# Gated linear attention: a head's square sum behind the next head's first projection, in another bank, and the next arguments ahead of the norm

## What is computed

```python
def _mixer_c(h, s0, with_state, w_in, w2, b2, norm_g, w_out):
    q, k, v, gz, lr = _split(h @ w_in, [H * GLA_DK, H * GLA_DK, H * GLA_DV, H * GLA_DV, 2 * GLA_RANK])
    ...
    o_f, s_f = _gla_chunked(q, k, v, glog[:, :, 0], s0[:, 0])
    o_b, s_b = _gla_chunked(_rev(q), _rev(k), _rev(v), _rev(glog[:, :, 1]), s0[:, 1])
    out = _gated_rms_norm(o_f + _rev(o_b), gz, norm_g) @ w_out

def _gated_rms_norm(o, z, g):
    y = o * lax.rsqrt(jnp.mean(o * o, axis=-1, keepdims=True) + EPS) * g.astype(F32)
    return (y.reshape(B, T, H * V) * jax.nn.silu(z.astype(F32))).astype(z.dtype)
```

## Time and profile before

| | us |
|---|---|
| timed executions, median of three | 1919.06 |
| their lowest and highest | 1918.38, 1927.1 |
| profiled execution, its time | 1928.48 |
| profiled execution, its span | 1926.7 |
| mean granted TensorE clock | 0.901 |

### The profile page before, as it was taken

The page is one execution under the profiler, slowest core; times in us unless marked ns, Lnnn a source line. Parts: engine busy times, 40 slices in busy tenths (PEclk is TensorE's granted clock), DMA queues, the critical chain, the costliest instruction groups (busy, mean ns, idle before and its releaser), DMA issues.

```text
span 1926.7 us, 21105 instructions
## 1 busy us (share of the span) xinstructions
PE 1687.5 (88%) x7872; PEld 1052.5 (55%) x7872; DVE 529.6 (27%) x1288; ACT 474.3 (25%) x865; POOL 147.6 (8%) x188
## 2 busy tenths in 40 slices
PE   5899999979998999798899999588898869999984
PEld 3455688865556888554543333456676545433334
DVE  1564332434634424202200000153232240000002
ACT  2254321222453212103111111143323131111111
POOL 0010011010000111000100000102222000000001
PEclk8899896889998968799899999787999889999997
DMA  9122125122123253015579999420210355999973
GB/s 373 51 82 87 67 110 200 42 110 83 72 88 140 105 211 144 26 44 209 221 306 402 406 398 412 134 104 11 103 44 5 142 240 214 367 407 403 393 304 105
DMA packets 65336, 354.80 MB, mean 184 GB/s; under 512 B 7952, under 2 KB 8208, under 8 KB 28240
## 3 DMA queue, kind: packets, MB, share of 16 engines
q1 hardware_dynamic: 47888, 316.70, 41.6%
q10 hardware_dynamic: 13888, 24.13, 3.7%
q0 software_dynamic: 3456, 12.58, 1.8%
HBM read 331.87 MB, written 27.27 MB: 186 GB/s over the span
## 4 chain that ended last, share of the span: by engine, by line
PE 73%; DMA 8%; DVE 7%; ACT 5%; issue 4%; SPq 1%; ACTq 0%; DVEq 0%; POOL 0%; POOLq 0%
PE bank L681 10%; PE bank L911 8%; PE bank L929 5%; PE bank L962 4%; PE bank L845 4%; DMA ring<-ws 4%; PE bank L780 4%; PE bank L764 4%; PE bank L1116 4%; DMA work<-ws 3%; PE bank L593 2%; PE bank L974 2%; PE bank L1182 2%; PE bank L788 2%; PE bank L1125 2%
## 5 line engine op out<-in xcount | busy, mean ns | idle before, releaser
L681 PE MATMUL bank<-hT,ring 128*128 128x384 f32 x768 | 261.4, 499 | 16.6 <-issue 10.6
L681 PEld LDWEIGHTS bank<-hT,ring 128*128 128x128 f32 x768 | 147.3, 195 | 122.2 <-issue 19.8
L1116 PE MATMUL bank<-hT,ring 128*128 128x384 f32 x256 | 92.7, 527 | 15.1 <-ACT work L1536 13.5
L911 PE MATMUL bank<-ring,work 128*128 128x512 f32 x192 | 90.6, 625 | 10.2 <-DMA ring<-ws 10.2
L911 PE MATMUL bank<-work 128*128 128x512 f32 x192 | 91.5, 631 | 6.1 <-DMA work<-ws 6.1
L2058 DVE TENSOR_TENSOR work<-bank,work 128x512 f32<-128x512 f32 x12 | 8.3, 693 | 309.6 <-PE bank L911 309.6
L845 PE MATMUL bank<-mix,ring 128*128 128x384 f32 x256 | 84.7, 495 | 8.7 <-DVE mix L1928 8.7
L593 PE MATMUL bank<-ring,small 128*32 128x256 f32 x768 | 66.5, 478 | 20.3 <-DMA ring<-ws 20.3
L1355 ACT ACTIVATE work<-bank 128x512 f32<-128x512 f32 x72 | 41.3, 597 | 172.3 <-PE bank L788 159.8
L780 PEld LDWEIGHTS bank<-work 128*128 128x128 f32 x576 | 78.6, 219 | 9.0 <-issue 9.0
L1116 PEld LDWEIGHTS bank<-hT,ring 128*128 128x128 f32 x256 | 52.7, 208 | 55.6 <-issue 16.6
(11 more groups left out here) (358 smaller groups left out, 2486.6 us busy)
## 6 DMA issues: line engine op xcount, KB each, us to landing
ring<-ws SPq DMA_DIRECT2D x192, 1024.0 KB, 9.0
work<-ws SPq DMA_DIRECT2D x96, 1024.0 KB, 13.7
y_slots<-work ACTq DMA_DIRECT2D x24, 256.0 KB, 6.3
x_slots<-s_gla SPq DMA_DIRECT2D x22, 256.0 KB, 6.6
work<-x_slots ACTq DMA_DIRECT2D x40, 128.0 KB, 6.8
y_slots<-work ACTq DMA_DIRECT2D x40, 128.0 KB, 7.6
work<-x_slots ACTq DMA_DIRECT2D x16, 256.0 KB, 8.0
work<-lruw_in ACTq DMA_DIRECT2D x8, 256.0 KB, 2.8
```

Of the source, the lines that this page charges most:

```text
L681: last = mm(bank[b % 2][:, 0:T], w[:, b % 2, k, :], hT[:, k, :], start=(k == 0), stop=(k == KD - 1))
L911: last = mm(bank[2 + kind][:], xg[p % 2][:, k, :], w[:, k % 4, :], start=(k == 0), stop=(k == KD - 1))
L1116: last = mm(bank[2 * i + m][:, 0:T], w[:, m, k, :], hT[:, k, :], start=(k == 0), stop=(k == KD - 1))
```

## The change

The loops over heads of TensorE and VectorE are written out (ScalarE's, GpSimd's and SyncE's stay loops). The square sum moves out of the head: `head_square(head)` waits for `osq` and sums in bank 6. It is called behind the first 8 projection matmuls of the next head, and, for the last head, behind six of the eight matmuls of the first output tile. The output projection starts with six matmuls each of tiles 0 and 1, which need only the first three heads, and finishes them behind `gomix` 4. The wait for `orstd` moves to a place inside the next head, behind its first scores; the first scores wait for four reads of the projections and no longer five. VectorE's arguments of the next head come ahead of its norm of this one. ScalarE's logarithm reads bank 6.

```diff
+                def head_square(head):
+
+                    pe.wait_ge(osq, head + 1 + HG)
+                    for j in range(2):
+                        last = mm(bank[6][:, 0:T], ones, gsq[:, j, :], start=(j == 0), stop=(j == 1))
+                    last.then_inc(oms, 1)
+
+                for g in range(2):
                     for hh in range(2):
...
                                 last.then_inc(gproj_done, 1)
+                                if i == 0 and m == 0 and g + hh:
+                                    head_square(2 * g + hh - 1)
...
-                        pe.wait_ge(gproj_read, g * 10 + (5 * hh + 5))
-                        pe.sem_inc(free[so + 2], 1)
+                        pe.wait_ge(gproj_read, g * 10 + (5 * hh + 4))
...
                         for d in range(2):
                             scores(6 * hh + d, glp[d], bank[d::2])
+                        pe.wait_ge(gproj_read, g * 10 + (5 * hh + 5))
+                        pe.sem_inc(free[so + 2], 1)
+                        if g + hh:
+                            pe.wait_ge(orstd, 2 * g + hh + HG)
...
-                        pe.wait_ge(osq, g * 2 + (hh + 1 + HG))
-                        for j in range(2):
-                            last = mm(bank[0][:, 0:T], ones, gsq[:, j, :], start=(j == 0), stop=(j == 1))
-                        last.then_inc(oms, 1)
-                        pe.wait_ge(orstd, g * 2 + (hh + 1 + HG))
+
+                for m in range(2):
+                    pe.wait_ge(loaded[0], 16 * (BASE["glaout"][0] + 1))
+                    w = slots[0].rearrange("p (m k c) -> p m k c", m=2, k=KD)
+                    if m == 0:
+                        pe.wait_ge(gomix, 3)
+                    for k in range(KD - 2):
+                        mm(bank[m][:, 0:T], w[:, m, k, :], mix[:, k, :], start=(k == 0), stop=False)
+                    if m == 0:
+                        head_square(3)
                 pe.wait_ge(gomix, 4)
...
-                    for k in range(KD):
+                    for k in range(KD - 2 if m < 2 else 0, KD):
...
-                        A(grstd, bank[0][:, 0:T], ACT.Ln, scale=1.0 / GLA_V, bias=cc("eps")).then_inc(ln_done, 1)
+                        A(grstd, bank[6][:, 0:T], ACT.Ln, scale=1.0 / GLA_V, bias=cc("eps")).then_inc(ln_done, 1)
...
-                with dve.Fori(0, 2) as g:
+                def head_arguments(g, hh):
+
+                    for d in range(2):
+                        last = copy_of(gch[:, d, :], gabs[:, g * 2 + (4 * d + hh), :])
...
+                head_arguments(0, 0)
+                for g in range(2):
                     for hh in range(2):
...
                         TT(gsq, go, go, ALU.mult).then_inc(osq, 1)
+                        if g + hh < 2:
+                            head_arguments(g + hh, 1 - hh)
                         dve.wait_ge(orstd, g * 2 + (hh + 1 + HG))
```

## The result

| | before | changed |
|---|---|---|
| first measurement: median, us | 1923.08 (4 executions, 1918.38 to 1928.66) | 1899.27 (4, 1892.43 to 1908.43) |
| its ratio | | 0.9886, 95% interval 0.9848 to 0.9925 |
| second: median | 1919.51 (23, 1910.55 to 1931.8) | 1893.20 (6, 1879.82 to 1916.26) |
| its ratio | | 0.9826, 0.9769 to 0.9883 |
| third: median | 1928.53 (11, 1908.62 to 1949.62) | 1882.67 (6, 1879.06 to 1910.77) |

All executions together (the spreads are standard deviations) give 1923.43 - 1893.45 = 30.0 us, 6.3 us either way, 1.6%. The ratios leave out slow executions, those over 1.5% above the fastest of the same kernel in the same measurement; without them the means are 1922.4 (52) and 1889.4 (14), 33.0 us apart.

The account below looks back on a forecast made before the run. TensorE was taken to bound the kernel (73% of the chain). Gains 9.9 + 8.8 + 9.6 + 6.2 = 34.5 us off 1928.5 give 1894.0, less 9.4 for the median: 1884.6; 8 in 10: 1876 to 1901.

Parts of the forecast that it names:

- head 0: First head of the GLA stage: no gain, since its score groups wait for GpSimd's products, which the change doesn't move.
- change 0 to 1: First change of head in the GLA stage: period falls from 54.8 to 44.9 us, a gain of 9.9.
- change 1 to 2: Second change of head: 55.0 us falls to 44.9 plus 1.3 waiting for head 2's weights, a gain of 8.8.
- change 2 to 3: Third change of head: period falls from 54.5 to 44.9 us, its weights being there; a gain of 9.6.
- output projection: End of the GLA stage: 54.2 us falls to 48.0 with one 3.0 us hole; gain 6.2, bounds 5 to 8.5.
- The clock loss behind the hole of 2.62 us: Output projection: slower clock after TensorE's idle time, forecast as a 3.0 us hole; 2.3 us taken, bounds 0 and 2.6.
- ScalarE and GpSimd: Chain feeding the next head's scores: last product ready at T0 + 34.0, due at T0 + 40.6, slack 6.6 us.
- T0: The end of a head's last attention matmul on TensorE, from which the forecast counts times and periods.
- The wait of 1.19 us: TensorE's wait for ScalarE's value copies ahead of the scores: goes, as scores wait only for the fourth projection read.
- Attention at the low clock: Rival, heads 1 to 3: 8.4 us lost per attention; gain 26.1 if one falls, 9.3 if all; chance 0.11.
- Slower through code: Rival: unrolled heads 2 and 3 need instruction packets, five stops of 10.56 us, giving 1937 us; chance 0.03.
- Another engine or the last experts' stream takes a part: Rival: product chain slips or last layer's weight stream doesn't move along; ten us lost, 1894.6 us; chance 0.08.

Follow-up runs that it names:

- phase_two: Changed kernel with two more 384-column matmuls (result not used) behind each of the first three square sums; GLA stage 238.8 us in one profile.
- wait_five: Changed kernel with the first scores again waiting for all five reads of the projections; GLA stage 245.8 us in one profile.
- unroll_only: Kernel before with only TensorE's and VectorE's loops over heads written out, no work moved; median 1927.53 us, ratio 1.0033 (0.9996 to 1.007).
- fuller: Changed kernel with six matmuls of a third output tile also ahead and weight loads one head earlier; stage 230.1 us, timed 1884.20 us, ratio 0.9777.
- args_late: Changed kernel with VectorE's arguments of the next head behind the norm again; GLA stage 235.8 us in one profile.
- old_out: Changed kernel with the output projection as before, all 64 matmuls behind the fourth product; stage 244.1 us, timed 1895.14 us, ratio 0.9856.
- phase_shift: Changed kernel with one more 384-column matmul (result not used) behind each of the first three square sums; GLA stage 238.2 us in one profile.
- phase_three: Changed kernel with three more 384-column matmuls (result not used) behind each of the first three square sums; GLA stage 243.0 us in one profile.
- fill_head0: Changed kernel with one unused 384-column matmul ahead of head 0's second and third score groups; GLA stage 237.2 us in one profile.
- after_third: Profile from the third measurement of the changed kernel, nothing altered; profiled at 1879.06 us, measurement's median 1882.67 us, ratio 0.9783.

## Why the prediction was right and wrong

**The stage, step by step**, in the first profiles:

| step | forecast | measured |
|---|---|---|
| head 0 | no gain | 56.0 to 54.8, gain 1.2 |
| change 0 to 1 | 44.9 | 44.3, gain 10.5 |
| change 1 to 2 | 46.2 with 1.3 for weights | 45.4 with 0.85, gain 9.6 |
| change 2 to 3 | 44.9 | 44.3, gain 10.2 |
| output projection | 48.0, hole 3.0 | 47.1, hole 2.62, gain 7.0 |
| sum | 34.5 | 38.5 |

The mechanisms that were named are there. The new periods were overestimated by 0.6 us each: the 32 projections take 20.6 us and not 20.9 (5.16 and 15.48, between the starts of the rows above), the attention 12.17 and not 12.3, and the attention's record overlaps the next projections by 0.17. The late weights were found from the time to landing in the earlier trace rows: 1.3 us forecast, 0.71 to 1.65 in four profiles. The clock loss behind the hole of 2.62 us, 2.3 assumed, is 35.37 - 33.6 = 1.8, and 1.4 against the 33.93 of phase_two. ScalarE and GpSimd: the last product of head 1 was ready at 1382.27 + 0.45 = 1382.72, T0 + 33.6, where T0 + 34.0 was forecast. The wait of 1.19 us is gone, and wait_five shows in one profile that its absence may be worth more than its length. Head 0, put at no gain, gained 1.2 us; its attention was 0.8 us shorter.

**The whole.** The step that failed is the last one: "Against the profiled execution's own 1928.5 us that is 1894.0", and then 9.4 less for the median. It takes some 1650 us of unchanged program as a constant. They are not constant. Ahead of the stage the profiles range from 1268.5 to 1294.2 with the same code, and the first profile of the changed kernel met the longest: 16.4 us of its stage's 38.5 went there. And the stage of the kernel before is not one number: 274 in three profiles, 263.9 in one. The base was low as well: 1919.06 is the median of three executions, and the mean of 54 is 1923.4; 34.5 below that is 1888.9. From the means of the four profiles of each kernel: before 1274.4 + 271.6 + 375.3 = 1921.3, changed 1277.0 + 233.4 + 377.3 = 1887.7. That is 38.2 gained in the stage and 2.6 and 2.0 lost around it, 33.6 in all, beside 30.0 (6.3 either way) over all executions. The forecast gain of 34.5 lies near the first and inside the second; it was the first four executions that were far from it. That it comes so near is partly luck: the stage gave 4 us more than the sum, and the rest took about as much back. Of those four only the one of 1908.43 us was profiled, so where the other three lost their time is not known. The text did warn that executions of one kernel lie some 8 us apart. It should have drawn from this that a difference of two medians of a few executions moves by 10 us.

**The rivals.** Attention at the low clock: not at heads 1 to 3 of the changed kernel (36 of 36 at 1.00 with its variants), but seen one edit away, where it cost 8.2 and 5.0 us for the price of 8.4. Slower through code: no stop of 10 us; the stage's waits name no issue. The Trainium skill, "Runtime: NRT & Kernel Launch" (Instruction fetch mechanics), says that straight code is fetched ahead of the engine, and the stage agrees. Behind the stage a small stop did appear, below. Another engine or the last experts' stream takes a part: 2.0 us behind the stage, and their cause is open. The new stop is 1.7 us long in the first profile, but the unrolled versions without it took 377.2 us behind the stage on average (four profiles), and those with it 377.3 (ten). The page "TensorE: Matmul & The Clock Gate" of the Trainium skill (HAM oscillation) would have let the last hole pass without a loss; the traces do not agree in nine of ten profiles, where the clock fell behind 2.62 us, and agree in one, phase_two. By the page the stage would have been forecast at 237.6 and not at 239.9 us; it came out at 235.9, nearer to the page, but by the shorter periods.

**What stays open.** Why head 0's attention runs at 0.61 to 0.67 in fourteen profiles and at 1.00 in four; the length of its projections sorts them, but that was not tried. Whether the changed kernel's wider spread (12.2 against 8.8) is chance or comes with the program. The group of 210.7 us was seen once, in a changed kernel, so that the kernel before meets it too is an inference from its times of up to 1950 us. The measurements ran on different chips, and the kernel before had medians of 1919.51 and 1928.53 on two of them: what the chip does and what chance does was not told apart. The executions of 1903 to 1916 us were timed only, but for the one at 1908.43, whose profile puts the loss ahead of the stage.

## What to carry to other kernels

A reduction that an engine needs only for the end of one unit can go behind the first matmuls of the next, into a bank that is idle; its worth is the hole, plus the clock that TensorE loses behind it, here about 2.7 of the 10.5 us of the first change of head (the projections took 23.34 us, start to start, and now take 20.64). Look at the loads before counting it: the next unit's weights were issued for the old start and were late by 0.7 to 1.7 us. Read a change's gain in its own stage of several profiles first, and expect a total to show it only when the rest, the same code, repeats within less than the gain.

## What the runs showed of the hardware

- The kernel before had executions between 1908.6 and 1950.3 us, and one stretch of mostly small matmuls took 184.5, 190.3 or 210.7 us in three profiles, with a granted clock between 235 and 450 us of 0.84, 0.81 and 0.74.
- A wait of 1 us ahead of a row of 32-column matmuls was followed by the low clock (0.58 and 0.70) in two of three cases in wait_five, and in none of fifteen in the kernel before and unroll_only. The same matmuls entered without a wait held 1.00 in 36 of 36. At head 0, filling 0.6 of 1.4 us of holes did not hold it.
- The same hole of 2.62 us was followed by a fall of the clock in nine profiles (35.37 to 35.50 us for 52 matmuls) and by none in a tenth, phase_two (33.93 us).
- TensorE can stop in straight code, and whether it does goes with the version of the kernel. In the last mean of squares (L622; L633 in fuller) the first stop, named as issue, is 5.2 to 5.7 us in every profile. A second one, 1.4 to 2.4 us long, appears in all four profiles of the changed kernel, in unroll_only, args_late, wait_five, old_out, fuller and fuller_timed, and in none of the kernel before nor in phase_shift, phase_two, phase_three and fill_head0. In after_third:

```profile
1857.62 6.92 PE L622 MATMUL bank<-hT,cst 128*128 128x128 f32 x44 [1.82 <-issue]
```

  At that line the versions are the same and differ in how much code of TensorE lies ahead. That the place of the code decides is a guess from this; it was not tried by itself.
